# S5 power tables by doubling, and another order of the rwkv side work beside mix_in

## The reference

```python
# block 1
h = rms_norm(x, norm_ffn1)
x = x + 0.5 * swiglu(h, ffn1_gate, ffn1_up, ffn1_down)
h = rms_norm(x, norm_mix)
p = h @ w_in                                   # "mix_in", 1792 rwkv and 768 attention columns
# rwkv7_time_mix, after a token shift of p
w = -softplus(-(w0 + tanh(w_lo) @ w2)) - 0.5
a = sigmoid(a0 + a_lo @ a2)
g = sigmoid(g_lo) @ g2                         # the output gates
kk = (k * k_k) / max(sqrt(sum_over_head((k * k_k)**2)), 1e-12)
k = k * (1.0 + (a - 1.0) * k_a)
bonus = sum_over_head(r * k * r_k) * v
...
# block 3, an S5 layer: per group a state of 64 complex numbers, discretised
# with its own step; the kernel uses powers 0 to 8 of the complex factor (16
# inputs a group, 128 partitions), and powers 8, 16, ... 64
```

## Time and profile before

| | |
|---|---|
| median of 3 runs (2859.18 to 2864.1) | 2861.3 us |
| profiled execution, its own time | 2866.69 us |
| its span, mean granted clock | 2864.9 us, 0.982 |
| TensorE busy | 2749.0 us, 96% |
| VectorE busy | 1417.7 us, 49% |
| ScalarE busy | 1005.4 us, 35% |
| GpSimd busy | 1164.9 us, 41% |

### The profile page before, as it was taken

One profiled execution on the slowest core, in us unless ns is written; L12 is line 12 of the kernel. 1 busy time (PEld: TensorE's weight loads), 2 busy tenths in 40 slices (PEclk: granted clock), 3 DMA queues, 4 the chain that ended last, 5 costly groups with the idle time before them and its releaser, 6 DMA issues. The chain is left out here.

```text
span 2864.9 us, 39149 instructions
## 1 busy us (share of the span) xinstructions
PE 2749.0 (96%) x16698; PEld 2243.3 (78%) x16698; DVE 1417.7 (49%) x1763; ACT 1005.4 (35%) x1388; POOL 1164.9 (41%) x511
## 2 busy tenths in 40 slices
PE   7899999899999999998999999998999999999997
PEld 6778887687888888777888888887887778888785
DVE  4975336675476436754615333105578545333422
ACT  4233224244333322446423333223325533222541
POOL 3334443553444444564444444444234424323342
PEclk9999999999999999999999999999999999999998
DMA  5444322100433332222223332335546212222232
GB/s 193 132 141 138 117 99 74 60 4 25 137 117 126 102 101 91 85 78 81 92 92 96 96 96 96 96 97 169 186 134 183 88 58 94 81 63 71 67 96 74
DMA packets 115213, 288.37 MB, mean 101 GB/s; under 512 B 34832, under 2 KB 46032, under 8 KB 114384
## 3 DMA queue, kind: packets, MB, share of 16 engines
q1 hardware_dynamic: 115040, 285.87, 31.4%
HBM read 261.94 MB, written 26.25 MB: 101 GB/s over the span
## 5 line engine op out<-in xcount | busy, mean ns | idle before, releaser
L428 POOL TENSOR_TENSOR weight_ring_r<-weight_ring,weight_hi_r 128x1024 fp32r<-128x1024 f32 (+2 forms) x412 | 1041.0, 2527 | 1582.6 <-ACT weight_hi_r L421 1582.6
L421 ACT ACTIVATE weight_hi_r<-weight_ring 128x1024 fp32r<-128x1024 f32 (+2 forms) x412 | 447.7, 1088 | 1477.2 <-PE acc L631 1091.9
L625 PE MATMUL acc<-p_r,weight_hi_r 128*128 128x512 f32 x1712 | 676.3, 395 | 21.8 <-DVE scr_r L680 13.5
L626 PE MATMUL acc<-scr_r,weight_hi_r 128*128 128x512 f32 x1120 | 441.7, 394 | 0.0
L631 PE MATMUL acc<-p_r,weight_ring_r 128*128 128x512 f32 x1712 | 420.9, 389 | 0.0
L625 PEld LDWEIGHTS acc<-p_r,weight_hi_r 128*128 128x128 f32 x1712 | 324.7, 190 | 93.7 <-ACT weight_hi_r L421 20.6
L626 PE MATMUL acc<-p_r,weight_hi_r 128*128 128x512 f32 x1008 | 392.2, 389 | 0.0
L631 PEld LDWEIGHTS acc<-p_r,weight_ring_r 128*128 128x128 f32 x1712 | 321.7, 188 | 66.9
L626 PEld LDWEIGHTS acc<-scr_r,weight_hi_r 128*128 128x128 f32 x1120 | 214.0, 191 | 46.6 <-issue 2.9
L625 PE MATMUL acc<-scr_r,weight_hi_r 128*128 128x512 f32 x544 | 220.1, 405 | 2.2 <-ACT weight_hi_r L421 2.2
L932 DVE SCALAR_TENSOR_TENSOR x<-acc,x 128x512 f32<-128x512 f32 x56 | 36.8, 687 | 373.8 <-PE acc L631 359.4
(11 more groups left out here) (554 smaller groups left out, 3960.5 us busy)
## 6 DMA issues: line engine op xcount, KB each, us to landing
weight_ring<-in_weights SPq DMA_DIRECT2D x372, 512.0 KB, 3.5
weight_ring<-in_weights SPq DMA_DIRECT2D x32, 704.0 KB, 4.0
weight_ring<-in_weights SPq DMA_DIRECT2D x8, 640.0 KB, 3.8
s_inner<-p SPq DMA_DIRECT2D x16, 256.0 KB, 4.4
s_outer<-p SPq DMA_DIRECT2D x16, 256.0 KB, 4.5
s_inputs<-p SPq DMA_DIRECT2D x16, 256.0 KB, 2.6
p<-s_inputs SPq DMA_DIRECT2D x8, 512.0 KB, 5.4
p<-s_inner SPq DMA_DIRECT2D x8, 512.0 KB, 6.9
```

Of the source, the lines that this page charges most:

```text
L421: self.nc.scalar.activation(self.r.weight_hi[:, ahead, 0:width], self.weight_ring[:, r, 0:width], ACT.Copy)\
L428: self.nc.gpsimd.tensor_tensor(rest, raw, hi, ALU.subtract).then_inc(self.weights_split, 1)
L625: pe.matmul(product.out(b, m), hi, op.hi(kx), start=kx == 0, stop=False)
L626: pe.matmul(product.out(b, m), hi, op.lo(kx), start=False, stop=False)
```

## The change

The power tables are built by doubling: with powers up to n there, the next n come from one set of wide instructions (n = 1, 2, 4), four multiplies into scratch and a subtract and an add. The reversed table is one copy instead of eight. The parts before the pieces are eight instead of nine and stand one or two each on blocks 1 to 7 (`ROW_DVE_AT`), where they stood on 1, 3, 4, 5 and 6.

Beside mix_in, TensorE takes the key sums ahead of output gates 2 and 3, one slot earlier, and the last bonus sums after slot 17 instead of 16. ScalarE squares the last keys a step earlier, takes the root ahead of `exps(0)` and output gates 2 and 3 after it. VectorE does `key_norms`, `keys(0)` and `keys(1)` ahead of `read(4)`, all `unit_keys` and `keys` ahead of `read(6)`, and `bonus(0)`, `bonus(1)` ahead of the rates.

```diff
--- before.py
+++ after.py
@@ -1107,8 +1107,8 @@
 
 
 MIX_ORDER = (6, 2, 3, 0, 1, 4, 5, 7, 8, 9)
-MIX_PE_AT = (3, 4, 5, 6, 7, 8, 9, 11, 13, 15, 16)
-MIX_ACT_AT = (2, 3, 4, 5, 6, 7, 8, 9, 10, 11, 13)
+MIX_PE_AT = (3, 4, 5, 6, 7, 8, 9, 11, 13, 15, 17)
+MIX_ACT_AT = (2, 3, 4, 5, 6, 7, 9, 10, 11, 13)
 MIX_POOL_AT = (16, 17, 18)
 RW_R, RW_K, RW_V, RW_SIG, RW_A, RW_G, RW_B, RW_KP, RW_BON, RW_SUM, RW_E1 = 0, 4, 8, 20, 24, 28, 32, 36, 40, 44, 48
 
@@ -1120,7 +1120,7 @@
 PI_BELOW = 3.1415925
 NG = 4
 PIECES = S5_G // NG
-ROW_DVE_AT = (1, 3, 3, 4, 4, 5, 5, 6, 6, *(8 + n // 2 for n in range(PIECES)))
+ROW_DVE_AT = (1, 2, 2, 3, 4, 5, 6, 7, *(8 + n // 2 for n in range(PIECES)))
 ROW_END = 16
 ROW_PE_AT, ROW_SP_AT = 19, 23
 EXP_AT, ANGLES_AT = 3, 5
@@ -1318,39 +1318,35 @@
         yield
         v.memset(tab[:, 0, 0, :], 1.0)
         then(v.memset(tab[:, 1, 0, :], 0.0))
-        for m in range(2, S5_L + 1):
-            xr, xi = tab[:, 0, m - 1, :], tab[:, 1, m - 1, :]
-            mul(th, xr, are)
-            mul(em, xi, aim)
-            mul(kf, xr, aim)
-            then(mul(t0, xi, are))
-            v.tensor_tensor(tab[:, 0, m, :], th, em, ALU.subtract)
-            then(v.tensor_tensor(tab[:, 1, m, :], kf, t0, ALU.add))
-            if m == 5:
-                yield
-        for n in range(S5_L):
-            ins = v.tensor_copy(rev[:, :, n, :], tab[:, :, S5_L - 1 - n, :])
-        ins.then_inc(q["tables"], 1)
+        flat = lambda a: a.rearrange("p a t -> p (a t)")
+        spare, places = flat(self.big), flat(self.steps)
+
+        def doubled(table, room):
+
+            for n in (1, 2, 4):
+                parts = [room[:, at * n * S5_G:(at + 1) * n * S5_G].rearrange("p (m g) -> p m g", g=S5_G) for at in range(4)]
+                xr, xi = table[:, 0, 0:n, :], table[:, 1, 0:n, :]
+                by = [table[:, c, n - 1:n, :].to_broadcast([P, n, S5_G]) for c in range(2)]
+                mul(parts[0], xr, by[0])
+                mul(parts[1], xi, by[1])
+                mul(parts[2], xr, by[1])
+                then(mul(parts[3], xi, by[0]))
+                v.tensor_tensor(table[:, 0, n:2 * n, :], parts[0], parts[1], ALU.subtract)
+                then(v.tensor_tensor(table[:, 1, n:2 * n, :], parts[2], parts[3], ALU.add))
+
+        doubled(tab[:, :, 1:, :], spare)
         yield
-        power8 = [self.big[:, r, :].rearrange("p (k g) -> p k g", g=S5_G) for r in range(2)]
-        are, aim = tab[:, 0, S5_L, :], tab[:, 1, S5_L, :]
-        v.tensor_copy(power8[0][:, 0, :], are)
-        then(v.tensor_copy(power8[1][:, 0, :], aim))
-        for k in range(1, 8):
-            xr, xi = (a[:, k - 1, :] for a in power8)
-            mul(th, xr, are)
-            mul(em, xi, aim)
-            mul(kf, xr, aim)
-            then(mul(t0, xi, are))
-            v.tensor_tensor(power8[0][:, k, :], th, em, ALU.subtract)
-            then(v.tensor_tensor(power8[1][:, k, :], kf, t0, ALU.add))
+        v.tensor_copy(rev, tab[:, :, S5_L - 1::-1, :]).then_inc(q["tables"], 1)
+        power8 = self.big.rearrange("p r (k g) -> p r k g", g=S5_G)
+        then(v.tensor_copy(power8[:, :, 0, :], tab[:, :, S5_L, :]))
+        doubled(power8, places)
+        yield
         for c, (source, sign) in enumerate(((0, 1.0), (1, -1.0), (1, 1.0))):
             to = self.steps[:, c, :].rearrange("p (h k j g) -> p h k j g", h=2, k=8, g=4)
-            by_half = power8[source].rearrange("p k (j h g) -> p h k j g", h=2, g=4)
+            by_half = power8[:, source].rearrange("p k (j h g) -> p h k j g", h=2, g=4)
             for half in range(2):
                 ins = v.tensor_scalar(to[:, half], by_half[:, half], sign, None, ALU.mult)
         ins.then_inc(q["tables"], 1)
-        yield
         v.tensor_scalar(x1, x1, core.const(1, "s5_sign"), None, ALU.mult)
         then(v.tensor_scalar(x2, x2, -1.0, None, ALU.mult))
         yield
@@ -1534,18 +1530,22 @@
                     mm(side_bank(1), lora[high, 1, at], p[high, LORA_W, :], start=True, stop=True).then_inc(q["lora"], 1)
                     yield
                 pe.wait_ge(q["sig"], PAIRS)
-                for i in range(PAIRS):
-                    if i >= 2:
-                        pe.wait_ge(q["g_read"], i - 1)
-                    mm(side_bank(i), lora[:, 2, i * P:(i + 1) * P], p[:, LORA_G, :], start=True, stop=True).then_inc(q["g_mm"], 1)
-                    if i % 2:
-                        yield
-                pe.wait_ge(q["g_read"], PAIRS)
+                out_gate = lambda i: mm(side_bank(i), lora[:, 2, i * P:(i + 1) * P], p[:, LORA_G, :], start=True, stop=True).then_inc(q["g_mm"], 1)
+                out_gate(0)
+                out_gate(1)
+                yield
+                pe.wait_ge(q["g_read"], 1)
                 for i in range(PAIRS):
                     pe.wait_ge(q["k_sq"], i + 1)
                     ins = mm(side_bank(0), C(f"gather{i}"), kp(i), start=(i == 0), stop=(i == PAIRS - 1))
                 ins.then_inc(q["k_sum"], 1)
                 yield
+                pe.wait_ge(q["k_inv"], 1)
+                pe.wait_ge(q["g_read"], 2)
+                out_gate(2)
+                out_gate(3)
+                yield
+                pe.wait_ge(q["g_read"], PAIRS)
                 pe.wait_ge(q["k_root"], 1)
                 for i in range(PAIRS):
                     if i >= 2:
@@ -1616,16 +1616,15 @@
                 key_squares((0, 1))
                 yield
                 gates(3)
+                key_squares((2, 3))
                 yield
                 out_gates((0, 1))
-                key_squares((2, 3))
-                yield
-                out_gates((2, 3))
-                yield
-                exps(0)
                 yield
                 act.wait_ge(q["k_inv"], 1)
                 a(p[:, 50, :], p[:, 50, :], ACT.Sqrt).then_inc(q["k_root"], 1)
+                exps(0)
+                yield
+                out_gates((2, 3))
                 exps(1)
                 yield
                 exps(2)
@@ -1765,32 +1764,34 @@
             bonus_start(0)
             bonus_start(1)
             sums(1)
+            key_norms()
+            keys(0)
+            keys(1)
             receptances(0)
             read(4)
             shift(4)
-            key_norms()
             bonus_start(2)
             bonus_start(3)
             sums(2)
             receptances(1)
             read(5)
-            shift(5)
             unit_keys(0)
             unit_keys(1)
+            shift(5)
             sums(3)
-            for i in range(PAIRS):
-                keys(i)
+            keys(2)
+            keys(3)
+            unit_keys(2)
+            unit_keys(3)
             receptances(2)
             read(6)
             shift(6)
-            unit_keys(2)
-            unit_keys(3)
             receptances(3)
+            bonus(0)
+            bonus(1)
             for i in range(PAIRS):
                 rates(i)
             read(7)
-            bonus(0)
-            bonus(1)
             read(8)
             bonus(2)
             bonus(3)
```

## The result

| | before | changed |
|---|---|---|
| median of 13 runs each, side by side | 2863.48 us (2859.09 to 2875.86) | 2852.36 us (2848.11 to 2862.01) |
| ratio, 95% interval | | 0.9963 [0.9953, 0.9973] |
| profiled execution, its span | 2866.69, 2864.9 us | 2851.17, 2849.4 us |

The change makes the kernel faster by 10.6 us (0.0037 x 2863.5; by the interval 7.7 to 13.5), where 14.8 were forecast. The time forecast, 2846.5, is 5.9 us too low: 2.2 of it because the median of before came out at 2863.5 and not at 2861.3, 3.7 because the gain is smaller (11.1 between the medians).

The account below looks back on a forecast made before the run. TensorE, busy for 96% of the span, was taken to bound the kernel with its own work plus gaps. 13.0 + 0 + 1.8 = 14.8 us off 2861.3 gave 2846.5 us; range 2836.5 to 2850.5, a little over 8 in 10.

Parts of the forecast that it names:

- Stalls 1 and 2: ffn1_up, slots 15 to 19: TensorE's two waits for a rounded weight slot go, gaining 13.0 us.
- The doubling: ffn1_up's power tables: rounds of 1.07, 1.5 and 2.3 us, 4.9 us per doubling; two take 9.8, 5.2 less than before.
- the reversed copy: ffn1_up's tables: eight reversing copies become one of 1024 columns, taken as 1.0 us.
- the reads of blocks 1 to 9: ffn1_up, VectorE: reads of blocks 5 to 7 were to come within 5 us of their products.
- mix_in: Slots 15 to 19: the bonus wait goes, a new 4.7 us stall stands ahead of slot 18; gain 1.8 us.
- The lower bound: mix_in: a gain of minus 1.5 us if two more holds strike.
- Stall 3: ffn1_up, row matmuls of pieces 2 and 3: wait kept, 0 us gained; 6.4 if gone, a rival at 15%.
- The base: Whole kernel: the median before the change, 2861.3 us, from which the 14.8 us gain was subtracted.

Follow-up runs that it names:

- the mix_in kernel: Kernel before with only the edits beside mix_in, tables as before: 2861.59 us, ratio 0.9993; mix_in's slots 15 to 19 took 32.25 us.
- Both cures of mix_in: Changed kernel with read(7) ahead of all four rates (2850.41 us), or with two rates ahead of the bonus and two behind read(7) (2844.56 us).
- changed again: The changed kernel itself, unaltered, run once more beside the kernel before: 2850.93 us, ratio 0.9954.
- third time: The changed kernel itself, unaltered, run a third time beside the kernel before: 2853.13 us, ratio 0.9959.
- the tables alone: Kernel before with only ffn1_up's edits (tables by doubling, spread over blocks 1 to 7), mix_in as before: 2856.13 us, ratio 0.9972.
- both cures: Changed kernel with two rates moved behind read(7) and SyncE's four table copies issued two slots later: 2842.18 and 2843.85 us, ratio 0.9934 twice.
- the rates split: Changed kernel with two rates ahead of the bonus, two behind read(7), GpSimd's side steps from slot 15: 2844.56 and 2848.60 us, ratios 0.9936 and 0.9946.
- the read first: Changed kernel with read(7) ahead of all four rates: 2850.41 us, ratio 0.9952.

## Why the prediction was off

**Stalls 1 and 2: right.** 13.0 us forecast. Measured 34.86 to 21.76; over the five profiles of the old ffn1_up (the mix_in kernel's with them), 34.55 on the mean, it is 12.8. The doubling was sized well (1.06, 1.5 and 2.3 us a round for 1.07, 1.5 and 2.3), the reversed copy took 0.68 for 1.0, and the reads of blocks 1 to 9 were at most 1.7 us late (block 10's was 4.35 late, behind stall 3's pieces).

**mix_in: right.** The forecast was a new stall of 4.7 us ahead of slot 18 behind read(7), 7.7 us with its slow matmuls, a gain of 1.8. The stall is 5.23 us, and the five profiles that have both halves and neither cure of mix_in, 33.0 to 33.5 us with a mean of 33.2, lie 8.0 above the 25.29 without it: against 35.1 a gain of 1.8 or 1.9. Both cures of mix_in, which keep the edit and only move the rates and the read, take the 8 us out of the stretch, so the place of the stall is shown. The lower bound was loosely made: two more holds of 2.1 make 1.8 into minus 2.4, not minus 1.5; nothing came near it. By the rule of the Trainium skill (SBUF — State Buffer, "SBUF: two separate sides") the lock is taken by whole instructions; the trace agrees: the 0.28 us add of 93.14 took 2.36 beside the pass of 92.85, and eight rate instructions of 0.68 took 11.3 us beside six GpSimd operations.

**Stall 3: this step failed.** "I take 0" for it rests on "so is the wait", read from one execution. The stall was seen in that one and is absent in the other four profiles of the old ffn1_up, while the changed one has it in seven of seven. So the term is not 0 but a loss of 4.2 us by the medians of the profiles (25.66 against 21.46). "The order and distances from slots 18 and 19 are unchanged" held for the transfer, which lands 7.6 to 7.9 us behind slot 19 in the changed profiles and 7.6 to 8.0 in the others. It did not hold for VectorE, which starts piece 2 0.37 us later behind the landing. The prediction saw that it was a near thing, with 1 us between stall and none, and bounded it only towards a gain; the loss belonged among the bounds, since one profile can't tell a wait that hangs on tenths of a microsecond from a constant one. With it the sum is 12.8 - 4.2 + 1.8 = 10.4, and the timed gains are 10.6, and 13.2 and 11.7 (changed again, third time). For the tables alone the sum is 8.6, timed 8.0. The intervals are 3 to 5 us to either side, so the timed runs alone would not tell 4.2 from 2.

**The base.** 2.2 us of the miss are the base: the median of three runs was 2861.3 and that of thirteen 2863.5. With that base the forecast would have been 2848.7, still 3.7 under the measured time, and those 3.7 are stall 3's. Between single profiles chance is larger than this: up to the end of slot 15 the changed tables' code took from 106.9 to 111.3 us, and what lies behind mix_in's slot 19, whose code is that of before, from 2305 to 2317.

**What stays open.** Why VectorE starts piece 2 0.46 us behind the landing with the spread parts and 0.1 without. And the largest stage sums are not fully paid: both cures come to 12.8 + 1.0 + 9.8 = 23.6, timed 18.9 twice (15.2 to 22.3). About 2.0 of that goes in the stage behind mix_in (above), which leaves 21.6, within the interval. A stall moved one block on in part of the executions could be the rest; that share was not measured. With the 2.0 the rates split alone comes to 16.4, timed 18.3 and 15.5. With the 4.9, and its own 26.69 us in slots 19 to 22, the read first comes to 12.5, timed 13.7.

Both cures together are the best version here: 2842.2 and 2843.9 us beside 2863.1 and 2864.3 of before, and 9.3 us under the changed kernel on one chip (2853.13 - 2843.85).

## What to carry to other kernels

Price a stall from slot end to slot end, and profile the same kernel more than once before a wait is entered as kept. Here work began within a microsecond of a competing instruction; the stall was there in one profile of five, and a shift of 0.37 us turned it on in all seven. When work moves into an engine's idle time beside a GpSimd pass, count the holds too, and ask what read the moved work now stands ahead of. Put work that nothing waits for behind the read that frees the matmul's banks, but not so far that its own consumer becomes late, and price the stage behind as well: of 8 us taken out of mix_in, 2.0 and 4.9 came back there.

## What the runs showed of the hardware

In the rows shown a GpSimd pass held the VectorE instruction with two inputs in SBUF that started while it ran, however short, so the price jumps: a lead of piece 2's start of 0.65 us or less gave two holds, 0.79 or more gave one, and between the two lay 4 to 5 us of TensorE's time in that stretch. Single-input copies were held too (the 64-column one of the earlier trace rows took 2.37 us beside the pass of 110.80), reads out of PSUM were not: those of line 980 that started inside a pass took 0.68 us. GpSimd pays as well: its pass took 2.82 us beside the rates (516.92) and 2.40 with VectorE idle (534.71). And a stall costs more than its length: in the changed kernel's mix_in the granted clock was 1.00 up to the wait (512.60 to 519.70) and 0.50, the lower of its two levels, from 524.97 to 529.00, where a matmul took 0.63 us instead of 0.39; from 533.00 on it was 1.00 again. So 5.23 us of waiting cost 8.0.
